# Two FFNs of a long kernel: gate and up columns by pairs of seven half-token products, both down halves last in each step

## What is computed

```python
for l in range(DEPTH):                       # two layers
    ...                                      # four mixing branches, merged, w_out
    h = rmsnorm(x, g_pre_ffn[l])
    f = (jax.nn.silu(h @ w_ffn_gate[l]) * (h @ w_ffn_up[l])) @ w_ffn_down[l]
    x = x + rmsnorm(f, g_post_ffn[l])
```

## Time and profile before

| | |
|---|---|
| time, median of 3 runs | 2735.32 us (2734.55 to 2737.93) |
| the profiled execution's own time | 2737.83 us |
| its span | 2736.1 us |
| PE, PEld busy | 99%, 82% |
| DVE, ACT, POOL busy | 50%, 42%, 53% |
| mean granted clock of TensorE | 0.996 |

### The profile page before, as it was taken

One profiled execution on the slowest core, in us unless ns is written; L12 is line 12 of the kernel. 1 busy time (PEld: TensorE's weight loads), 2 busy tenths in 40 slices (PEclk: granted clock), 3 DMA queues, 4 the chain that ended last, 5 costly groups with the idle time before them and its releaser, 6 DMA issues.

```text
span 2736.1 us, 36369 instructions
## 1 busy us (share of the span) xinstructions
PE 2696.2 (99%) x13190; PEld 2230.5 (82%) x13190; DVE 1372.5 (50%) x1811; ACT 1148.5 (42%) x1756; POOL 1457.2 (53%) x1094
## 2 busy tenths in 40 slices
PE   9999999999999999999999999999999998999999
PEld 7878787888887788887888877789998876789998
DVE  6745455222248654555221268676554237466552
ACT  4444434322243444434222247544444337554442
POOL 5455545444464545455445455467774432358773
PEclk9999999999999999999999999999999999999999
DMA  4223222222232222222222232232233220123232
GB/s 145 93 93 108 98 87 85 100 93 100 94 108 93 95 98 100 100 93 85 93 100 95 98 99 89 86 105 93 100 100 128 80 84 17 61 96 105 93 100 100
DMA packets 72715, 259.38 MB, mean 95 GB/s; under 512 B 8192, under 2 KB 9088, under 8 KB 72448
## 3 DMA queue, kind: packets, MB, share of 16 engines
q1 hardware_dynamic: 71280, 254.17, 27.6%
q10 hardware_dynamic: 1296, 3.28, 0.3%
HBM read 255.31 MB, written 2.10 MB: 94 GB/s over the span
## 4 chain that ended last, share of the span: by engine, by line
PE 69%; issue 13%; POOL 11%; DVE 4%; ACT 2%; DMA 1%; POOLq 0%; SPq 0%; DVEq 0%
PE ps L1101 21%; PE ps L1102 21%; PE ps L1103 20%; POOL w_lo L438 6%; POOL w_lo L436 5%; PE ps L1369 1%; DMA w_raw<-w_all 1%; PE ps L1264 1%; DVE st L1831 1%; PE ps L1135 1%; PE ps L1129 1%; PE ps L1130 1%; PE ps L1255 1%; PE ps L1714 1%; PE ps L1716 1%
## 5 line engine op out<-in xcount | busy, mean ns | idle before, releaser
L436 POOL TENSOR_TENSOR w_lo<-w_raw,w_hi 128x512 fp32r<-128x512 f32 x432 | 592.3, 1371 | 1118.5 <-ACT w_hi L534 1118.1
L1101 PE MATMUL ps<-H_hi,w_hi 128*128 128x512 f32 (+1 forms) x1984 | 771.5, 389 | 7.8 <-POOL w_lo L438 4.7
L1103 PE MATMUL ps<-H_hi,w_lo 128*128 128x512 f32 (+1 forms) x1984 | 755.0, 381 | 0.0
L1102 PE MATMUL ps<-H_lo,w_hi 128*128 128x512 f32 (+1 forms) x1984 | 754.6, 380 | 0.0
L534 ACT ACTIVATE w_hi<-w_raw 128x1024 fp32r<-128x1024 f32 x454 | 477.5, 1056 | 547.7 <-DMA w_raw<-w_all 546.0
L438 POOL TENSOR_TENSOR w_lo<-w_raw,w_hi 128x512 fp32r<-128x512 f32 x432 | 595.0, 1377 | 0.0
L1101 PE MATMUL ps<-Y_hi,w_hi 128*128 128x512 f32 x1168 | 458.8, 393 | 9.5 <-DVE Y_lo L1979 6.3
L1102 PE MATMUL ps<-Y_lo,w_hi 128*128 128x512 f32 x1168 | 455.9, 390 | 0.0
L1103 PE MATMUL ps<-Y_hi,w_lo 128*128 128x512 f32 x1168 | 455.2, 390 | 0.0
L1101 PEld LDWEIGHTS ps<-H_hi,w_hi 128*128 128x128 f32 x1984 | 373.6, 188 | 95.0 <-issue 14.8
L1102 PEld LDWEIGHTS ps<-H_lo,w_hi 128*128 128x128 f32 x1984 | 373.7, 188 | 76.4 <-issue 7.4
(11 more groups left out here) (329 smaller groups left out, 3653.1 us busy)
## 6 DMA issues: line engine op xcount, KB each, us to landing
w_raw<-w_all SPq DMA_DIRECT2D x476, 512.0 KB, 3.2
X<-xT SPq DMA_DIRECT2D x8, 256.0 KB, 5.3
rel_bias<-bias ACTq DMA_DIRECT2D x1, 2048.0 KB, 10.1
outT<-X SPq DMA_DIRECT2D x8, 256.0 KB, 2.0
sguw<-sgu_wT ACTq DMA_DIRECT2D x2, 256.0 KB, 3.3
CS<-cossin SPq DMA_DIRECT2D x1, 256.0 KB, 7.6
sgub<-sgu_b ACTq DMA_DIRECT2D x2, 128.0 KB, 3.0
sgug<-sgu_g ACTq DMA_DIRECT2D x2, 128.0 KB, 3.2
```

What stands on the lines that cost most here:

```text
L436: nc.gpsimd.tensor_tensor(w_lo[:, s, 0:UNIT // 2], w_raw[:, s, 0:UNIT // 2], f(w_hi[:, s, 0:UNIT // 2]), ALU.subtract).then_inc(w_lo_half, 1)
L1101: MM(out, wh, xh, start=start, stop=False, skip_group_check=resumed)
L1102: MM(out, wh, xl, start=False, stop=False, skip_group_check=resumed)
L1103: return MM(out, wl, xh, start=False, stop=stop, skip_group_check=resumed)
```

## The change

Per layer 14 of the 22 hidden tiles have their gate and up columns made as a pair by seven half-token products. Tiles 0 to 3 are made as before, tiles 4 and 5 as plain units inside steps 0 and 1, tiles 6 to 19 in the pair steps 2 to 15, tiles 20 and 21 as before. Each of the 16 steps ends with two down halves (4 k-tiles of 512 columns each, one unit); the last eight down units have 6 k-tiles. Units, loads and down matmuls stay as many. Unlike the MLP's, a step has its seven products one behind another and both down halves behind them.

```diff
@@ TensorE
-                ffn(8, U["ffn"], 0, SPLIT[f"ffn{l}"], 4)
-                ffn(8, U["ffn"], 1, SPLIT[f"ffn{l}"])
-                ffn(6, U["ffn"] + 48, None, SPLIT[f"ffn{l}"] + 16)
+                def window(w):
+                    u, q = window_unit(l, w), ffn_pair(l, w)
...
+                    pe.wait_ge(w_lo_half, u + 2)
+                    if w == FFN_PLAIN:
+                        pe.wait_ge(unit_out, u - 1)
+                        pe.wait_ge(t_lo_v, 4 * l + 4)
+                    else:
+                        pe.wait_ge(g_c, 2 * q)
+                    half_product(BANK_Q, *slot_part(u + 1, 1), *half_of_h(4, 0))
+                    pe.wait_ge(w_lo_ready, u + 1)
+                    half_product(BANK_G, *slot_part(u, 1), *tokens(3)).then_inc(w_used, 1)
+                    pe.wait_ge(unit_out, u)
+                    half_product(BANK_R, *slot_part(u + 1, 0), *half_of_h(0, 0)).then_inc(w_used, 1)
+                    pe.wait_ge(w_lo_ready, u + 2)
+                    half_product(BANK_V, *sum_part(w, S1_), *tokens(0)).then_inc(g_mm, 1)
+                    pe.wait_ge(g_lo, 3 * q + 2)
+                    pe.wait_ge(g_copy, 4 * q + 2)
+                    half_product(BANK_R, *sum_part(w, S2_), *tokens(1), fresh=False).then_inc(g_mm, 1)
+                    pe.wait_ge(g_lo, 3 * q + 3)
+                    pe.wait_ge(g_copy, 4 * q + 3)
+                    half_product(BANK_V, *sum_part(w, S4_), *half_of_h(4, 1), fresh=False).then_inc(g_mm, 1)
+                    pe.wait_ge(g_copy, 4 * q + 4)
+                    half_product(BANK_R, *sum_part(w, S3_), *tokens(2), fresh=False).then_inc(g_mm, 1)
+                    half_down(0)
+                    half_down(1)
@@ ScalarE
+                def window(w):
+                    last = w == FFN_WINDOWS - 1
+                    copied(w, COPY_G)
+                    copied(w, COPY_R1)
+                    if last:
+                        hi(window_unit(l, w, 3))
+                    else:
+                        hi_second(w + 1)
+                    copied(w, COPY_V)
+                    hi(window_unit(l, w, 4))
+                    if not last:
+                        hi_sum(w + 1, S1_, 1)
+                        hi_sum(w + 1, S3_, 2)
+                        hi(window_unit(l, w, 5))
+                    copied(w, COPY_R2)
+                    if not last:
+                        hi_sum(w + 1, S2_, 3)
+                        hi_sum(w + 1, S4_, 4)
+                    gated(w)
+                    product_hi(4 + w, 0, 4 * ((1 + w // 4) % 2) + w % 4)
@@ VectorE
+                def weight_sum(w, o):
...
+                    if q:
+                        dve.wait_ge(g_mm, 4 * (q - 1) + {S1_: 1, S3_: 0, S2_: 2, S4_: 3}[o] if q > 1 or o != S3_ else 1)
...
+                def window(w):
...
+                    if not last:
+                        weight_sum(w + 1, S1_)
+                        weight_sum(w + 1, S3_)
+                        weight_sum(w + 1, S2_)
+                        weight_sum(w + 1, S4_)
+                    dve.wait_ge(g_copy, 4 * q + 4)
+                    dve.wait_ge(g_mm, 4 * q + 3)
...
+                tile(5, window_unit(l, 1), 6, 7, 5)
+                low_tokens(l, 1, 3)
+                weight_sum(FFN_PLAIN, S3_)
+                weight_sum(FFN_PLAIN, S2_)
+                weight_sum(FFN_PLAIN, S4_)
+                down(1, 0)
+                down(1, 1)
+                dve.wait_ge(unit_out, window_unit(l, 1, 3))
+                low_tokens(l, 2, 4)
```

More of the change, by code:

```diff
@@ L501, in _ @@
                 at = u0 + 4
+                if name.startswith("pre_ffn"):
+                    l = int(name[-1])
+                    lows(at, window_unit(l, FFN_PLAIN))
+                    for w in range(FFN_PLAIN, FFN_WINDOWS):
+                        low_gated(l, w)
+                    at = window_unit(l, FFN_WINDOWS)
             lows(at, UM0 + 4 + 4 * PLAIN)
@@ new lines, in _ @@
+                U0 = U["ffn"]
+                for j in range(4):
+                    swish(j, j)
+                    if j < 3:
+                        tick(U0 + 4 + j)
+                    product_hi(j, j, j)
+                    if j == 2:
+                        tick(U0 + 7)
+                    tokens_split(j)
+                    if j == 3:
+                        tick(U0 + 8)
+                        tick(U0 + 9)
+                swish(4, 4)
+                tick(U0 + 10)
+                product_hi(4, 4, 4)
@@ L1414, in attended, with half_product, tokens, half_of_h @@
                         m.then_inc(w_used if e else part_mm, 1)
+            def half_product(bank, wh, wl, xh, xl, fresh=True):
+                for k in range(4):
+                    c = slice(k * P, (k + 1) * P)
+                    m = three(ps[:, bank, 0:HS], wh[:, c], wl[:, c], xh(k), xl(k), fresh and k == 0, k == 3, not fresh)
+                return m
+            def tokens(t):
+                return (lambda k: T_hi[:, t, k, :]), (lambda k: T_lo[:, t, k, :])
+            def half_of_h(k0, h):
+                r = slice(h * HS, (h + 1) * HS)
+                return (lambda k: H_hi[:, k0 + k, r]), (lambda k: H_lo[:, k0 + k, r])
             pe.wait_ge(consts_made, 6)
@@ L1535, in _ @@
             gemm(UAO + 3, DT - 3, Yh, Yl)
[L1537 to L1549, removed]
             def mlp(n, U0):
@@ new lines, in plain, with down @@
+                def plain(t, u, y):
+                    tile(t, u, u % 4, (u + 1) % 4, y)
+                def down(w, d):
+                    m, b = 2 * (w % 4) + d, (U0 + 2 * (w % 2) + d) % 4
+                    if d:
+                        dve.wait_ge(w_used, window_unit(l, w, 3))
+                    else:
+                        dve.wait_ge(g_dmm, FFN_WINDOWS * l + w + 1)
+                    by, n = (unit_out, window_unit(l, w, 1)) if d else (g_dout, FFN_WINDOWS * l + w + 1)
+                    if w < 4:
+                        VE.tensor_copy(Dn[:, m, :], ps[:, b, :]).then_inc(by, 1)
+                    else:
+                        VE.tensor_tensor(Dn[:, m, :], Dn[:, m, :], ps[:, b, :], ALU.add).then_inc(by, 1)
+                    if not d:
+                        dve.wait_ge(by, n)
@@ new lines, in _ @@
+                plain(0, U0, 0)
+                plain(1, U0 + 2, 1)
+                token_sums(l, 0)
+                plain(2, U0 + 4, 2)
+                token_sums(l, 1)
+                plain(3, U0 + 6, 3)
+                token_sums(l, 2)
+                tile(4, window_unit(l, 0), 4, 5, 4)
+                token_sums(l, 3)
+                down(0, 0)
+                down(0, 1)
+                dve.wait_ge(unit_out, window_unit(l, 0, 3))
+                low_tokens(l, 3, 1)
+                low_tokens(l, 0, 2)
```

339 lines of the change are left out of this document (240 added, 99 removed).

## The result

| | before | after |
|---|---|---|
| time, median | 2736.11 us (2734.55 to 2737.93, 4 runs) | 2804.01 us (2797.68 to 2805.34, 4 runs) |
| ratio | | 1.0247, 95% interval 1.0234 to 1.0259 |
| profiled execution, span | 2737.83, 2736.1 us | 2797.68, 2795.9 us |
| mean granted clock | 0.996 | 0.990 |

What follows compares the result with a forecast made beforehand. TensorE, busy 99% of the span, was taken as the bound. Matmuls -22.9, wait before S3 +35.1, first pairs +11.2 and clock +3.2 gave +26.6 us, predicting 2762 us; range 2745 to 2790 for 8 in 10.

Steps and rivals of the forecast that it cites:

- Matmuls: TensorE, gate and up pairs: seven half products take 10.06 us where two units took 10.88; 22.9 us saved over both layers.
- The wait before S3: Pair steps: the seventh product waits for ScalarE's copy of S2 out of its bank, 1.35 us in 26 steps, 35.1 us.
- 0.15 us to spare: Pair steps: the down unit's load lands at 8.28 us, ScalarE comes to it at 8.43.
- The bound of 2.3 us: Upper bound of the wait before the seventh product in a step, where 1.35 us was taken and 1.05 was the lower.
- The first pairs: Start of each layer's first pair: product Q waits for GpSimd's second gate half, 5.6 us, twice, 11.2 us (8.8 to 14).
- The upper bound of 7.0 us: Delay of a layer's first pair if GpSimd's operations take 2.36 us each, as in an MLP's first pair.
- The clock: Behind each layer's first pair: a lower granted clock costs 1.6 us, twice, 3.2 us (0 to 6); nothing added in the steps.
- My sign of being wrong: Pair steps: among the signs against the forecast, a granted clock below 1.00 throughout them.
- the clock falls in every step: Rival, pair steps: the wait before S3 grows to 1.89 us, each of 26 costs 1.6, 41 more: 2803 us; chance 0.08.
- Edits costed at nothing: Token sums, GpSimd's nine operations, VectorE's and ScalarE's step work and the loads were all taken as hidden, 0 us.
- the copy is not late: Rival, pair steps: S3 waits little, so the other terms win; with no wait -8.5 us, 2727 us; chance 0.06.

Runs made afterwards that it cites:

- e8: e7 with each layer's first pair prepared sooner on VectorE, ScalarE and GpSimd, and TensorE waiting for each token sum only at its product; 2727.30 us, ratio 0.9969.
- e11: e8 with GpSimd making the first pair's low parts of S2, S4 and S3 before both halves of the first down unit; 2721.14 us, ratio 0.9953.
- e5: The changed kernel with three extra float32 matmuls on TensorE between product S4 and the wait before S3; 2790.19 us, ratio 1.0196.
- e1: The changed kernel with the copy S3 waits for moved on ScalarE to just behind the gate unit's split; 2749.54 us, ratio 1.0051.
- e7: e1 with VectorE evacuating the step's two down halves before it forms the tile's low part; 2730.28 us, ratio 0.9980.
- e12: The changed kernel with e7's early evacuation alone, the copy staying behind the down unit's split on ScalarE; 2799.10 us, ratio 1.0239.

## Why the prediction missed, step by step

*Matmuls, -22.9: right.* Free of waits a step takes 15.54 us where three units took 16.3: 0.78 per pair, and the predicted 0.82 within reading.

*The wait before S3, +35.1: the mechanism right, the size wrong.* It measured 2.07 us a step, not 1.35, and 53.8 in all. The term that failed is "0.15 us to spare" for the down unit's load. It rested on one MLP step, whose load came 4.09 us after R's last matmul; in the pair steps after, it took 5.1 on average, so the load came up to 1.47 us too late for ScalarE (0.94 in the step shown). That the row stood for little could have been read from the trace before. Over the 22 pair steps of the two MLPs this load landed 4.07 to 6.49 us after R's last matmul, 4.72 on average, and the step of the rows is one of the two earliest. VectorE's sum in that step waited 0.71 us for the same load (its timeline):

```profile
1909.04 1.21 DVE L2298 TENSOR_TENSOR E_raw<-E_raw,w_raw 128x512 f32<-128x512 f32 x1 [0.71 <-DMA w_raw<-w_all]
```

The group of all such sums had 25.4 us of such waits, 1.27 us for each of the 20 that waited. With the mean of 4.72 the load is 0.48 us late where it had 0.15 to spare, and the wait comes to an estimated 1.8 us. Why the load took another 0.4 us in the new steps is not shown. The slow sum S3, to which I gave 0.15 us, set the end only in a few steps. The bound of 2.3 us held the value; my middle did not.

*The first pairs, +11.2: right.* 10.8 us idle, by the releaser named. e8, which moves work on VectorE, ScalarE and GpSimd together, and e11, which moves GpSimd's alone, take 6.4 of it away by order. The upper bound of 7.0 us is a slip: three operations at 2.36 us behind 16.8 end at 23.9, 7.6 us late. Nothing else rests on it.

*The clock, +3.2: wrong.* Behind the first pairs it was 4.8. In the steps I added nothing because a wait of 1.2 us lay below both of the earlier trace rows; at 1.92 it does not, and the steps lost 15.4 us. This term, put at nothing, is what carried the time out of the range: with 53.8 us for the wait and nothing for the clock in the steps, the same sum gives 2781. My sign of being wrong, a clock below 1.00 throughout the pair steps, came in part: 9 of 26. The rival "the clock falls in every step" had the condition right and came within 1 us by number (2803), but its 41 us assumed a drop in all 26 steps, with 35.1 for the wait: that it came out is luck, two errors that cancel. e5 shows that the idle time is the cause.

*Edits costed at nothing: half right.* GpSimd and the token sums cost nothing: in the kernel after no pair step but a layer's first waits for GpSimd, and no plain tile waits for a token sum. VectorE's evacuation of the second half was put at 1 us into the next step, ahead of R's place at 2.9; in e1 R waited 0.48 us for it. It was hidden only because the late copy lengthened the step; e1, e7 and e12 show it worth 20 us once the copy is early. So the rival "the copy is not late" would have been wrong too: 2749.5, not 2727, with the copy early alone.

## What to carry to other kernels

A copy that frees an accumulator is short, but in an engine that runs in order it is as late as the slowest load ahead of it: put it ahead of everything that waits for a transfer. For a transfer with little to spare, take the mean and spread of its group, not one row. When a wait is removed, compare every circle between two engines with the matmuls' own time, since the next one may be only 0.8 us shorter.

## What the hardware showed that was not expected

In the steps the clock did not fall in the idle time but behind it, in all nine cases. In the kernel after, S3 restarted at 611.25 with matmuls at 0.12 us as before the wait. From 612.3 on they took 0.21, the down half's 0.43, and from 615.6 again 0.23; these are pieces of the chain (start, us, what):

```profile
612.11 0.18 PE ps L1238
612.29 0.21 PE ps L1236
...
613.58 0.43 PE ps L1236
...
615.64 0.23 PE ps L1238
```

Nor does the length of the idle time decide alone. Here are a longer wait, 2.15 us at 1391.90, and a shorter one, 1.73 us at 1409.42, in TensorE's timeline, and then the stretch around each:

```profile
1391.90 0.39 PE L1236 MATMUL ps<-T_hi,G_hi 128*128 128x256 f32 x1 [2.15 <-ACT XS L860]
...
1409.42 0.39 PE L1236 MATMUL ps<-T_hi,G_hi 128*128 128x256 f32 x1 [1.73 <-ACT XS L860]
```

```profile
1390.00:1396.00 6.00, 4.09 (x24) 3.65 (x25) 5.32 (x8) 3.00 (x5) 6.00 (x4) 1.00 0.02 3
1408.00:1414.00 6.00, 4.58 (x19) 4.00 (x20) 5.83 (x7) 3.00 (x5) 6.00 (x4) 0.73 0.00 0
```

The longer wait left the clock at 1.00, the shorter one was followed by 0.73. What decides between two such steps these runs don't show.

VectorE's sums of two SBUF inputs took 0.69 us where nothing was ahead of them and 1.56 behind a GpSimd operation. In e1_copy_first (VectorE, then GpSimd):

```profile
601.83 0.69 DVE L2341 TENSOR_TENSOR G_raw<-w_raw 128x512 f32<-128x512 f32 x1
602.66 1.56 DVE L2344 TENSOR_TENSOR G_raw<-G_raw,w_raw 128x512 f32<-128x512 f32 x1
...
602.05 1.62 POOL L495 TENSOR_TENSOR w_lo<-w_raw,w_hi 128x512 fp32r<-128x512 f32 x1 [1.86 <-DVE G_raw L2338]
```

The sum ended at 604.22, 0.55 us after GpSimd's operation (603.67). The Trainium skill, page "SBUF — State Buffer", section "SBUF: two separate sides", says that a VectorE operation with two SBUF inputs and a GpSimd operation lock each other out of one port pair for a whole instruction. By that the sum would have ended at 603.67 + 0.69 = 604.36; the trace agrees to 0.14 us.
